# Transposing the first pass's activations on TensorE instead of through HBM

## The chip, the cores and the metric

The kernel runs on the 8 cores of one Trainium2 chip. Each core computes one half of one of the four sequences, 4096 tokens, and no data passes between cores. The metric is the time of one execution in microseconds, set by the slowest core. Lower is better.

## What is computed

The reference is a decoder block on x of shape (4, 8192, 1024):

```
h      = rms_norm(x);  proj = h @ w_in                   # 1024 -> 5888 columns
y_a    = (B * causal_conv3(C * v)) @ w_proj_a            # short gated convolution
y_b    = attention in 3 groups of 4 heads (dilation 1, 4, 16; 128 keys back) @ w_proj_b
x      = x + (sigmoid(g_a) * y_a + sigmoid(g_b) * y_b) @ w_out
h2     = rms_norm(x)
x      = x + (silu(gate) * val) @ w_down                 # gate, val = causal_conv3(h2 @ w_up)
out    = rms_norm(x)
```

A matmul on TensorE sums over partitions. So the normalised rows h, which are made with tokens on partitions, have to be transposed (channels on partitions) before they can be multiplied with w_in.

## The kernel before

Every core works in three passes. **Pass A** (to about 450 us of the trace) normalises the rows, transposes them, projects q, k and v and runs the attention, whose sums go to a tensor `u_d` in HBM. **Pass B**, the mixer (about 450 to 1070 us), projects the convolution's inputs and the gates from the same h, combines the branches and multiplies with w_out. **Pass C** is the gated MLP. TensorE, VectorE (DVE), ScalarE (ACT), GpSimd (POOL) and SyncE (SP) each run their own list of instructions in order, with waits on semaphores. SP issues nearly all DMAs, in order too: while SP waits for one transfer's condition, everything behind it in its list waits. The weights are loaded from POOL's list.

Pass A goes over tiles of 512 tokens in the order 0, -1, -2, 1, E, -3, 2, -4, 3, 4, 5, 6, 7. Tiles 0 to 7 are the core's own tokens. Tiles -4 to -1 and the 16 rows of E lie before them and give only keys and values. A tile is four blocks of 128 rows, and one list `NBL` holds all blocks in order. Each block goes through three steps that are written between the tiles' matmuls:

- `stat(i)`: ACT squares and sums a row (L405), and POOL makes the reciprocal root from it with six small instructions (L319 to L327).
- `mul(i)`: DVE multiplies the block with it (L413) into one of four buffers `hbA`. Then SP issues the x load of block i+4 (L366), which needs the buffer that `mul(i)` has just read, and a store of the block's rows to the HBM tensor `h_d` (L468).
- `back(i)`: brings the block, transposed, into `hTA`, one of four tiles. Two ways exist. For tile 0 and E, `norm_back` runs eight TensorE transposes of 128x128 into one PSUM bank (L425) and one DVE copy out of it (L429). For all other tiles, SP issues one transposing DMA from `h_d` into `hTA` (L484), which waits until the store has landed.

What paces these steps is a counter of ticks: `tick()` is called after each small group of matmuls (usually 8), 20 times in one of the tiles 0 to 7, 16 times in tile -1, 6 or 7 times in -2, -3 and -4. `norm_tick` does at most one `back`, one `mul` and one `stat` in a tick: a new block every 2.4 ticks (every 3.3 from block 24 on), a `mul` at least two ticks after its `stat`, a `back` at least 3 ticks after its `mul` where TensorE transposes and 4 where a DMA does. A tile starts only when its four blocks' `back` steps are written (`need`).

The matmuls of pass A go through L643 (`fm`) and L649 (`tm`). They and `norm_back` take the next of four PSUM banks from `next_ps`; the results leave the banks through `copy` (L256 on ACT, L258 on DVE), and `pick` sends each to the engine with the smaller sum of noted costs. The attention adds scores (L530), exponentials (L533), masks (L537) and products with the values (L556). Group 2's values take a detour through the HBM tensor `v2_d` (`v_d` in the profile: stored at L735, loaded at L740) on SP's list.

Pass B reads h again, from `h_d`, by 33 transposing DMAs of its own (`hb_load`, L984); it needs the rows of tiles 0 to 7 and the last four rows before them. Pass C does the same through `h2_d` (33 more; the profile calls both tensors `h_d`). Pass B transposes its attention output on TensorE in groups of six (L1088).

Of the kernel before, what the change touches and what calls it, by code (L numbers as in the profile page):

```python
# [131 lines left out]
def build_program():  # L132
# [197 lines left out]
    def scale_g(gap, key):  # L330

        S.add("act", lambda e: e.activation(out=gap, in_=gap, func=AF.Copy, scale=float(D) ** 0.5 * RC ** 3 / 2), reads=[key], writes=[key])
# [25 lines left out]
    def emit_xload():  # L358
        i = xload_i[0]
        if i >= len(NBL):  # L360
            return
        xload_i[0] += 1
        t, b = NBL[i]
        n = 16 if t == "E" else 128
        r0, sl = x_row(t, b), i % 4
        S.add("sp", lambda e: e.dma_start(out=xA[sl][0:n, :], in_=x_loc[r0:r0 + n, :]),  # L366
              writes=[("xA%d" % sl,)], dma_sem=sem_x[sl])
# [44 lines left out]
    def norm_mul(xap, xkey, hbap, hbkey, n, gb, gkey, col):  # L412
        S.add("dve", lambda e: e.scalar_tensor_tensor(  # L413
            out=hbap[0:n, :], in0=xap[0:n, :], scalar=rstd[0:n, col:col + 1], in1=gb[0:n, :],
            op0=ALU.mult, op1=ALU.mult), reads=[xkey, ("rstd", col), gkey], writes=[hbkey])
        note("dve", 1450)
# [32 lines left out]
        stamp["s", i] = tickno[0]  # L449

    def by_pe(t):
        return t in ("E", 0)

    def h_row(t, b):
        return 2048 + 512 * t + 128 * b

    def mul(i):
        t, b = NBL[i]
        n = 16 if t == "E" else 128
        if not g1_scaled[0]:  # L460
            g1_scaled[0] = True
            scale_g(g1b, ("g1b",))
        hb, hk = hbA[i % 4], ("hbA%d" % (i % 4),)
        norm_mul(xA[i % 4], ("xA%d" % (i % 4),), hb, hk, n, g1b, ("g1b",), cols_a[i])
        emit_xload()
        if t != "E":
            r0 = h_row(t, b)
            S.add("sp", lambda e: e.dma_start(out=h_d[r0:r0 + 128, :], in_=hb), reads=[hk], writes=[("h_d", t, b)],  # L468
                  dma_sem=sem_ha[i % 4])
        stamp["m", i] = tickno[0]  # L470

    def back(i):
        t, b = NBL[i]
        hk = ("hbA%d" % (i % 4),)
        if t == "E":
            norm_back(hbA[i % 4], hk, 16, hTE, ["hTE"])
            return
        sl = slot_of[t]
        dst, dk = hTA[sl][:, :, b * 128:(b + 1) * 128], [("hTA%d" % sl, b)]
        if by_pe(t):  # L480
            norm_back(hbA[i % 4], hk, 128, dst, dk)
            return
        r0 = h_row(t, b)
        S.add("sp", lambda e: e.dma_start(out=dst, in_=h_d[r0:r0 + 128, :], transpose=True), reads=[("h_d", t, b)],  # L484
              writes=dk, dma_sem=sem_ht[sl][b])

    def norm_tick(force=False):
        if nt[0] < nm[0] and (force or tickno[0] - stamp["m", nt[0]] >= (3 if by_pe(NBL[nt[0]][0]) else 4)) and can_back(nt[0]):
            back(nt[0])
            nt[0] += 1  # L490
        if nm[0] < ns[0] and (force or tickno[0] - stamp["s", nm[0]] >= 2) and nm[0] - nt[0] < 4:
            mul(nm[0])
            nm[0] += 1
        if nt[0] == len(NBL) and 4 in done_tiles and not normed[0]:
            normed[0] = True
            later(1, load_conv)
        ncred[0] = min(ncred[0] + (1 / 2.4 if ns[0] < 24 else PACE), 1.5)
        if ns[0] < len(NBL) and ns[0] - nm[0] < 2 and (force or ncred[0] >= 1):
            ncred[0] -= 1
            stat(ns[0])  # L500
            ns[0] += 1
# [1232 lines left out]
```

## Time and profile before

| | us |
|---|---|
| median of 3 runs (2065.27 to 2070.92) | 2068.2 |
| the profiled execution's own time | 2060.88 |
| its span on the slowest core, 5 | 2059.3 |
| its spans on the other cores | 2039.2 to 2055.6 |

The span runs from a core's first instruction to its last; 1.6 us of the profiled execution lie outside the slowest span. The profiled execution lies 7.3 us under the median. The rows further down are core 5's unless they say core 7. "PE" is TensorE, "PEld" its weight loads, "SPq" the DMA issues of SP. `arena` is the SBUF area that holds nearly all buffers, `psp` is PSUM, `x_loc` the input.

### The profile page before, as it was taken

What the parts mean: (1) busy time and instruction counts of PE and PEld (TensorE: products, weight loads), DVE (VectorE), ACT (ScalarE), POOL (GpSimd) and SP (SyncE); (2) the same over time, 40 slices, a digit from 0 to 9 for tenths busy, and PEclk for the clock granted to TensorE, in tenths of its full rate; (3) what the DMA queues carried; (4) which work ended last, traced back from release to release, by engine and by line L of the source; (5) the groups of instructions that cost most, each with busy time, mean ns of one, the idle gap of its engine ahead of it and who ended that gap; (6) DMA issues with size and microseconds to landing.
All of it is one profiled execution on the core that took longest, in us unless ns stands there. A gap on an engine that the chain in (4) does not pass through costs nothing.

```text
span 2059.3 us, 37750 instructions; the slowest of 8 cores (2039.2 to 2059.3 us)
## 1 busy us (share of the span) xinstructions
PE 1958.0 (95%) x11582; PEld 1011.7 (49%) x11582; DVE 1141.9 (55%) x1774; ACT 811.9 (39%) x1659; POOL 660.5 (32%) x1429
## 2 busy tenths in 40 slices
PE   4789889999999999999999999999999999999998
PEld 2456455655555544444444545555444444444443
DVE  3345454456344445345333938667684867758483
ACT  2344455453222221121222726446462635446361
POOL 2453322001111210110224425445452634445242
PEclk9899999999999999999999999999999999999999
DMA  9999988475333614123449941322313222221201
GB/s 214 167 233 203 218 219 161 102 163 139 112 101 106 118 56 134 39 96 111 62 127 181 197 111 22 103 69 87 112 48 91 74 67 83 57 93 46 83 1 52
DMA packets 224717, 229.54 MB, mean 111 GB/s; under 512 B 123060, under 2 KB 177466, under 8 KB 224136
## 3 DMA queue, kind: packets, MB, share of 16 engines
q1 hardware_dynamic: 182408, 192.73, 34.7%
q0 software_dynamic: 42112, 34.39, 12.2%
q8 instruction: 98, 1.61, 0.3%
q14 instruction: 99, 0.81, 0.1%
HBM read 162.29 MB, written 70.80 MB: 113 GB/s over the span
## 4 chain that ended last, share of the span: by engine, by line
PE 80%; DMA 8%; issue 4%; DVE 3%; POOL 2%; ACT 2%; SPq 1%; DVEq 0%; POOLq 0%; ACTq 0%
PE psp L643 54%; PE psp L1488 14%; PE psp L1243 6%; PE psp L649 3%; DMA h_d<-arena 3%; DMA arena<-w_in 2%; DVE arena L1445 2%; PE psp L556 1%; PE psp L530 1%; SPq L484 1%; ACT arena L1438 1%; ACT arena L405 1%; PE psp L1088 1%; DMA arena<-h_d 0%; DMA arena<-u_d 0%
## 5 line engine op out<-in xcount | busy, mean ns | idle before, releaser
L643 PE MATMUL psp<-arena 128*128 128x512 bf16 (+4 forms) x6848 | 1349.7, 358 | 39.3 <-DMA arena<-h_d 15.3
L643 PEld LDWEIGHTS psp<-arena 128*128 128x128 bf16 x6848 | 660.0, 98 | 689.3 <-issue 55.8
L1445 DVE SCALAR_TENSOR_TENSOR arena<-psp,fcw_s,arena 128x511 f32<-128x511 f32 (+4 forms) x792 | 520.0, 686 | 98.6 <-ACT uc L1436 34.8
L1488 PE MATMUL psp<-arena 128*128 128x512 bf16 x1408 | 308.7, 380 | 5.9 <-POOL arena L1449 2.8
L1438 ACT ACTIVATE arena<-psp,fcb_s,fcw_s 128x512 f32<-128x512 f32 (+1 forms) x396 | 282.8, 733 | 0.0
L1458 POOL TENSOR_TENSOR arena<-arena 128x512 bf16<-128x512 bf16 (+1 forms) x198 | 210.3, 1063 | 76.5 <-ACT uc L1436 48.2
L405 ACT ACTIVATE arena<-arena 128x1024 bf16<-128x1024 f32 (+1 forms) x114 | 120.0, 1053 | 278.4 <-DVE arena L1514 247.2
L1488 PEld LDWEIGHTS psp<-arena 128*128 128x128 bf16 x1408 | 137.8, 98 | 175.0 <-issue 12.4
L1211 DVE TENSOR_TENSOR arena<-psp,arena 128x512 f32<-128x512 f32 (+2 forms) x144 | 90.7, 632 | 219.6 <-PE psp L643 210.9
L1197 ACT ACTIVATE arena<-psp,bg_s 128x512 f32<-128x512 f32 (+2 forms) x144 | 92.0, 640 | 275.0 <-PE psp L643 269.8
L1456 ACT ACTIVATE arena<-arena 128x512 bf16<-128x512 f32 (+1 forms) x198 | 115.4, 583 | 183.2 <-POOL arena L1449 167.8
L1215 POOL TENSOR_TENSOR arena<-arena 128x512 bf16<-128x512 f32 (+2 forms) x72 | 83.5, 1160 | 280.6 <-DVE arena L1211 220.7
L1449 POOL TENSOR_TENSOR arena<-arena,corr 128x2 f32<-128x2 f32 x352 | 89.2, 257 | 179.3 <-DVE arena L1445 166.7
L319 POOL TENSOR_SCALAR ssq<-ssq 128x1 f32<-128x1 f32 (+1 forms) x110 | 27.7, 252 | 366.6 <-ACT arena L405 320.3
L1514 DVE TENSOR_TENSOR arena<-psp,arena 128x512 f32<-128x512 f32 x64 | 43.7, 690 | 178.3 <-PE psp L1488 178.2
L413 DVE SCALAR_TENSOR_TENSOR arena<-arena,rstd 128x1024 bf16<-128x1024 f32 (+1 forms) x82 | 107.0, 1305 | 47.8 <-POOL rstd L327 46.1
L649 PE MATMUL psp<-arena 128*128 128x256 bf16 (+1 forms) x952 | 121.0, 286 | 13.1 <-DMA arena<-h_d 11.2
L256 ACT ACTIVATE arena<-psp 128x512 bf16<-128x512 f32 (+3 forms) x116 | 63.0, 544 | 170.2 <-PE psp L643 114.3
L537 DVE TENSOR_TENSOR arena<-arena,mask 128x1024 bf16<-128x1024 bf16 x96 | 66.1, 689 | 108.1 <-ACT arena L533 108.0
L1243 PE MATMUL psp<-arena 128*128 128x512 bf16 (+1 forms) x528 | 118.1, 382 | 2.5 <-POOL arena L1215 2.5
L533 ACT ACTIVATE arena<-psp 128x1024 bf16<-128x1024 f32 x96 | 96.6, 1020 | 45.8 <-PE psp L530 41.2
L649 PEld LDWEIGHTS psp<-arena 128*128 128x128 bf16 (+1 forms) x952 | 97.0, 106 | 28.0 <-issue 13.8
(85 smaller groups left out, 975.2 us busy)
## 6 DMA issues: line engine op xcount, KB each, us to landing
arena<-x_loc SPq DMA_DIRECT2D x80, 512.0 KB, 5.9
arena<-x_d SPq DMA_DIRECT2D x64, 512.0 KB, 3.7
h_d<-arena SPq DMA_DIRECT2D x80, 256.0 KB, 6.2
x_d<-arena SPq DMA_DIRECT2D x32, 512.0 KB, 3.7
out<-arena SPq DMA_DIRECT2D x32, 512.0 KB, 2.6
u_d<-arena SPq DMA_DIRECT2D x96, 132.0 KB, 5.0
arena<-u_d SPq DMA_DIRECT2D x32, 396.0 KB, 4.1
arena<-w_up POOLq DMA_DIRECT2D x22, 512.0 KB, 14.8
```

The lines of the kernel that those rows point to most:

```text
L405: S.add("act", lambda e: e.activation(out=junk[0:n, :], in_=xap[0:n, :], func=AF.Square, accum_out=ssq[0:n, col:col + 1]), reads=[xkey] + ...
L413: S.add("dve", lambda e: e.scalar_tensor_tensor(out=hbap[0:n, :], in0=xap[0:n, :], scalar=rstd[0:n, col:col + 1], in1=gb[0:n, :], op0=ALU. ...
L533: S.add("act", lambda e: e.activation(out=PA[pi], in_=psp[pr], func=AF.Exp, scale=0.125), reads=[("ps", 2 * pr), ("ps", 2 * pr + 1)], writ ...
L643: S.add("pe", lambda e, kc=kc: e.matmul(out, lhsT=wap[:, kc, col0:col0 + 128], rhs=rhs(kc), start=(kc == 0), stop=(kc == kcn - 1), skip_gr ...
L649: S.add("pe", lambda e, kc=kc: e.matmul(out, lhsT=lhs(kc), rhs=wap[:, kc, c0:c0 + n], start=(kc == 0), stop=(kc == KC - 1), skip_group_che ...
L1197: S.add("act", lambda e, b=b, t=t, br=br: e.activation(out=tmp[t][:, 0:w_], in_=ps[b][:, 0:w_], func=AF.Sigmoid, bias=bg[:, br * 8 + oc:br ...
L1243: S.add("pe", lambda e, b=b, kc=kc, hf=hf: e.matmul(ps[b][0:n, :], lhsT=mT[:, kc, c0:c0 + n], rhs=wO[kc // 4][:, kc % 4, hf * 512:(hf + 1) ...
L1438: S.add("act", lambda e, b=b, t=t, ch=ch, w2_=w2_: e.activation(out=tmpC[t][:, 0:n], in_=ps[b][:, o:w_], func=AF.Identity, scale=w2_, bias ...
L1445: S.add("dve", lambda e, b=b, t=t, sh=sh, wv_=wv_, lo=lo: e.scalar_tensor_tensor(out=tmpC[t][:, lo:n], in0=ps[b][:, o + lo - sh:w_ - sh], ...
L1456: S.add("act", lambda e: e.activation(out=actT[:, p, 0:n], in_=tmpC[tg][:, 0:n], func=AF.Silu), reads=[("tmpC%d" % tg,)], writes=[("actT", ...
L1458: S.add("pool", lambda e: e.tensor_tensor(out=actT[:, p, 0:n], in0=actT[:, p, 0:n], in1=tmpC[tv][:, 0:n], op=ALU.mult), reads=[("tmpC%d" % ...
L1488: S.add("pe", lambda e: e.matmul(ps[b], lhsT=actT[:, k_, bi * 128:(bi + 1) * 128], rhs=wt[:, kk, hf * 512:(hf + 1) * 512], start=(k_ == 0) ...
```

## The change

Every block of pass A is now transposed on TensorE: `by_pe` is true for all tiles, so `back` always calls `norm_back`, three ticks after `mul`, and no transposing DMA (L484) is issued in pass A. The store to `h_d` stays for tiles 0 to 7 and for the last block of tile -1, which pass B reads; tiles -4, -3, -2 and the first three blocks of -1 are no longer stored. Pass B's transposing loads stay as they were.

```
--- before.py
+++ after.py
@@ -449,7 +449,7 @@
         stamp["s", i] = tickno[0]
 
     def by_pe(t):
-        return t in ("E", 0)
+        return True
 
     def h_row(t, b):
         return 2048 + 512 * t + 128 * b
@@ -463,7 +463,7 @@
         hb, hk = hbA[i % 4], ("hbA%d" % (i % 4),)
         norm_mul(xA[i % 4], ("xA%d" % (i % 4),), hb, hk, n, g1b, ("g1b",), cols_a[i])
         emit_xload()
-        if t != "E":
+        if t != "E" and (t >= 0 or (t, b) == (-1, 3)):
             r0 = h_row(t, b)
             S.add("sp", lambda e: e.dma_start(out=h_d[r0:r0 + 128, :], in_=hb), reads=[hk], writes=[("h_d", t, b)],
                   dma_sem=sem_ha[i % 4])
```

## Rows read from the trace of the kernel before

**Rows 1.** The page's first line, and its busy times by engine.

```profile
span 2059.3 us, 37750 instructions; the slowest of 8 cores (2039.2 to 2059.3 us)
...
PE 1958.0 (95%) x11582; PEld 1011.7 (49%) x11582; DVE 1141.9 (55%) x1774; ACT 811.9 (39%) x1659; POOL 660.5 (32%) x1429
```

**Rows 2.** Waits of TensorE, 0 to 500 us: total, times, longest.

```profile
PE psp L643 <- DMA arena<-h_d: 15.3, 2, 13.8
...
PE psp L649 <- DMA arena<-h_d: 11.2, 2, 7.4
...
PE psp L643 <- DMA arena<-w_in: 9.1, 2, 5.8
...
PE psp L556 <- DMA arena<-v_d: 6.0, 1, 6.0
...
PE psp L643 <- ACT arena L256: 2.6, 1, 2.6
```

**Rows 3.** Timeline of SP's queue, tile 3: start, length, what is issued.

```profile
272.88 1.22 SPq L484 DMA_TRANSPOSE arena<-h_d  x1
...
274.79 0.39 SPq L735 DMA_DIRECT2D v_d<-arena  x1
...
280.25 0.32 SPq L740 DMA_DIRECT2D arena<-v_d  x1
```

**Rows 4.** Timeline of ScalarE: start, length, work, [idle before <- releaser].

```profile
207.18 1.06 ACT L405 ACTIVATE arena<-arena 128x1024 bf16<-128x1024 f32 x1 [6.72 <-DMA arena<-x_loc]
```

**Rows 5.** Timeline of TensorE, the work right after its long waits.

```profile
84.44 6.70 PE L643 MATMUL psp<-arena 128*128 128x128 bf16 x32 [13.83 <-DMA arena<-h_d]
...
123.48 7.74 PE L649 MATMUL psp<-arena 128*128 128x256 bf16 x56 [3.78 <-DMA arena<-h_d]
...
208.95 3.31 PE L643 MATMUL psp<-arena 128*128 128x512 bf16 x8 [2.61 <-ACT arena L256]
...
231.23 4.97 PE L649 MATMUL psp<-arena 128*128 128x256 bf16 x24 [7.39 <-DMA arena<-h_d]
...
288.75 3.60 PE L649 MATMUL psp<-arena 128*128 128x256 bf16 x16
```

**Rows 6.** The same view, the mixer: transposes among matmuls.

```profile
586.53 0.50 PE L1088 MATMUL psp<-ident,arena 128*128 128x128 bf16 x6
...
586.86 7.07 PE L1243 MATMUL psp<-arena 128*128 128x512 bf16 x32
```

**Rows 7.** Groups by line, 0 to 500 us: count, busy, mean ns, idle before.

```profile
L425 PE MATMUL psp<-ident,arena 128*128 128x128 bf16 (+1 forms) x40 | 4.4, 277 | 19.1 <-DVE ssq L319 16.6 <-DVE arena L413 2.5
...
L429 DVE COPY arena<-psp 128x1024 bf16<-128x1024 bf16 x4 | 2.7, 683 | 1.3 <-PE psp L425 1.3
```

**Rows 8.** Instructions on h_d: count, ns min/median/max, first and last start.

```profile
L468 SPq DMA_DIRECT2D h_d<-arena x48: 336/424/1527, 11.9 to 331.1; - x48
...
L484 SPq DMA_TRANSPOSE arena<-h_d x44: 1216/1484/6877, 38.9 to 337.9; - x44
```

**Rows 9.** Busy us by engine in one stretch, clock, DMA share, GB/s.

```profile
294.00:448.00 154.00, 153.65 (x1545) 91.84 (x1544) 77.51 (x135) 78.79 (x109) 19.51 (x37) 1.00 0.68 139
```

**Rows 10.** Timeline of VectorE: the multiply of a block of 128 rows.

```profile
68.49 1.28 DVE L413 SCALAR_TENSOR_TENSOR arena<-arena,rstd 128x1024 bf16<-128x1024 f32 x1
...
98.00 1.28 DVE L413 SCALAR_TENSOR_TENSOR arena<-arena,rstd 128x1024 bf16<-128x1024 f32 x1 [2.30 <-POOL rstd L327]
...
101.55 1.28 DVE L413 SCALAR_TENSOR_TENSOR arena<-arena,rstd 128x1024 bf16<-128x1024 f32 x1 [1.34 <-POOL rstd L327]
```

**Rows 11.** Waits of TensorE on core 7, 0 to 500 us.

```profile
PE psp L643 <- DMA arena<-h_d: 12.2, 2, 11.7
...
PE psp L649 <- DMA arena<-h_d: 10.4, 2, 5.4
...
PE psp L556 <- DMA arena<-v_d: 4.2, 1, 4.2
```

**Rows 12.** Span and mean clock of core 7.

```profile
core 7: 2055.6 us, clock 0.985
```

More of the change, by code:

```diff
@@ L451, in by_pe @@
     def by_pe(t):
-        return t in ("E", 0)
+        return True
     def h_row(t, b):
@@ L465, in mul @@
         emit_xload()
-        if t != "E":
+        if t != "E" and (t >= 0 or (t, b) == (-1, 3)):
             r0 = h_row(t, b)
```

## The prediction

> **What bounds the kernel now.** I read the page first, then TensorE's waits in pass A, then what stands behind each of them in the lists of SP and ACT. On the page TensorE is busy for 1958.0 of 2059.3 us [rows 1], so a microsecond is won only where TensorE stands still, and every microsecond of work added to TensorE counts. The waits of pass A show where it stands still: 26.5 us in four waits for transposing loads from h_d (15.3 and 11.2), 9.1 us for weights, 6.0 us for group 2's values and 2.6 us for an eviction on ACT [rows 2].
>
> The last two have the same root. SP's list is in order, and a transposing load in it holds everything behind it until its block's store has landed. At 272.88 us such a load goes out; only then, at 274.79, the store of group 2's values, and their load at 280.25 [rows 3], for which TensorE waits 6.0 us. ACT stands still for 6.72 us until 207.18 because an x load sat in the same list [rows 4]; the eviction behind that `stat` is the one for which TensorE waits 2.6 us. So 26.5 + 6.0 + 2.6 = 35.1 us on core 5 hang on the round trip through h_d.
>
> After each long wait TensorE is also slow. In pass B, at a granted clock of 1.00, the level of 2.4 GHz, 32 matmuls of 512 columns take 7.07 us [rows 6]: 0.22 us each, 0.11 for 256 columns, 0.055 for 128. After the waits the rows read [rows 5]: 6.70 us for 16 matmuls of 128 and 16 of 512 columns (the line names one form), where 4.4 is the full rate; 7.74 for 56 of 256 against 6.2; 3.31 for 8 of 512 against 1.8; 4.97 for 24 of 256 against 2.65; 3.60 for 16 of 256 against 1.8. That is 2.3 + 1.5 + 1.5 + 2.3 + 1.8 = 9.4 us lost at the lower level, 1.2 GHz. Standstill and slow restart together: 44.5 us on core 5.
>
> **The added transposes.** Eleven tiles of four blocks change over: 44 groups of eight transposes on TensorE. The same instruction in pass B shows the cost among matmuls: six start at 586.53, the next matmul starts at 586.86 [rows 6], so 0.055 us each and 0.44 us for eight. 44 x 0.44 = 19.4 us. The lower bound is 18.5, if the first two groups, which fall among the waits for weights in tile 0, cost nothing. The upper is 39, twice 19.4, at the lower of the two clock levels. I take 19.4, since most groups fall where TensorE runs dense.
>
> **The added copies.** 44 copies of 0.68 us [rows 7], 30 us of DVE. In the densest stretch, 294 to 448 us, DVE is busy for 77.51 of 154 us and ACT for 78.79 [rows 9]. The copies also raise DVE's noted cost, so `pick` sends about half as many microseconds of other evictions to ACT. I cost them at nothing, covered by the other three of the four PSUM banks. Without that cover each group would hold TensorE for its copy, 0.68 us, 30 us in all (the slow rival below).
>
> **The removed DMAs.** 44 transposing loads, each holding SP for 1.2 to 6.9 us, and 15 of 48 stores go [rows 8]. The x loads, u_d stores and v2 stores behind them move up. All 35.1 us of waits lose their cause. From below, nothing is left of the gain from SP if the 33 remaining stores, which still wait for DVE, hold it as long; they wait for the same `mul` as the x load ahead of them, so I don't expect that. Two stores and two transposing loads of 256 KB each also vanish from the first 51 us, where TensorE waits 9.1 us for weights [rows 2]: 0 to 9 us, and I take 3, since the weights' own bytes remain.
>
> **The moved wait.** A transposing DMA let TensorE go on with other work; a TensorE transpose that is early stops its whole in-order list, and behind it the evictions and the next `stat`s. Two places matter. Tile -1's last block: its multiply runs from 68.49 to 69.77 [rows 10]. Counting ticks, its transposes come at the last but one tick of tile 0, before a last group of 8 x 0.22 us; tile 0 ends at 84.44 - 13.83 = 70.6 [rows 5], so TensorE is there at about 68.8 and waits 1 us instead of 13.8. Then tiles -1 and -2: multiplies come 3.55 us apart (98.00, 101.55), each just behind POOL's reciprocal root [rows 10]. Tile -1's matmuls at full rate sum to 18.5 us in 16 ticks; with transposes that is some 1.3 us a tick, 3.2 us per block of 2.4 ticks. TensorE is thus 0.35 to 0.6 us per block faster than the chain, over nine blocks 3 to 5 us. I take 6 for both places. Bounds: 0, and 16 if thirteen blocks each wait for the whole multiply, 1.28 us. Later tiles have longer ticks (8 matmuls of 512 columns, 1.8 us, and attention between), so the chain stays ahead.
>
> **The sum, core by core.** Core 5: 44.5 - 19.4 - 6 + 3 = 22.1 us less, 2037.2. But the slowest core counts, and core 5 suffers most now. Core 7 spans 2055.6 [rows 12]; its waits are 12.2 + 10.4 + 4.2 = 26.8 [rows 11], and with slow restarts in core 5's proportion (26.8 x 9.4 / 35.1 = 7.2) 34.0 us. It gains 34.0 - 19.4 - 6 + 3 = 11.6 and ends at 2044.0, after core 5. The slowest span falls by 15.3, the profiled execution from 2060.9 to 2045.6. That execution lay 7.3 us under the median, so the forecast for the median is 2068.2 - 15.3 = 2052.9, or 2053.
>
> **A rule that speaks against it.** The Trainium skill (TensorE: Matmul & The Clock Gate, Part 4) puts a transpose at about 275 ns in a kernel's context. By its figure 352 of them would cost an estimated 97 us instead of 19.4. The mean of 277 ns in tile 0 and E [rows 7] agrees with it as a duration; as a price among matmuls the trace disagrees, since durations overlap there [rows 6].
>
> **Rivals.**
> - *The norm chain paces TensorE.* The wait for h_d becomes a wait for the multiply at its bound of 16 us, with some 2 us of slow restart: 12 us worse, 2065. For it: the 3.55 us pace. Against: it holds for nine blocks only, and the plan leaves three ticks.
> - *Slower: PSUM.* A group of transposes takes one of four banks, and its copy can go to DVE alone, behind multiplies that wait for POOL. If TensorE waits for each copy, 44 x 0.68 = 30 us more: 2083. It decides the sign from 15.3 / 44 = 0.35 us per group. Against it: the half idle DVE [rows 9].
> - *Slower: transposes don't overlap.* At the 0.22 us that one lasts at the full clock (0.50 us for six starting 0.055 apart leaves 0.22 for the last), 352 x 0.22 = 77 us, 58 more: 2111. Against it: the starts 0.055 apart [rows 6]. The page's figure above would end here.
> - *The change does half of what it says.* SP stays clogged by the 33 stores; on core 7 the 4.2 us wait and its restart remain: 2058. Inside the forecast's range.
>
> **How the numbers follow.** Forecast, with its unknown costs (2040 to 2062): 0.77. Norm chain: 0.13. PSUM: 0.08. No overlap: 0.02. A measurement of this kernel can tell about 0.3%, 6.2 us, from no change: 2062.0 to 2074.4. All of the forecast is faster; of the norm chain I give 0.01 to faster, 0.11 to the same and 0.01 to slower; the PSUM case is slower but for 0.02, which a mild form leaves within the bound. So faster 0.78, same 0.13, slower 0.09. For the range I go from 2039 (no new stall, 6 us more from the weights, a little run to run) to 2067, past the norm chain's time; what lies above is the two slower cases and a few hundredths.
>
> **What would show it.** Right: no L484 left in pass A; 392 matmuls at L425 that start some 0.055 us apart; TensorE's wait for h_d below 500 us gone, and with it the waits for v_d and for ACT near 207 us; tile 1 starting some 15 us before 123.5; tile 0's end a few microseconds before 70.6. Wrong: L425 waiting for L413 for more than about 10 us (norm chain); L643 or L649 waiting for L429, or for evictions in the dense stretch that has none now (PSUM); a granted clock below 1.00 between 294 and 448 us; or the slowest core gaining much less than its own waits add up to, which would say that time is lost again in passes B or C.

## The result and the profile after

The changed kernel takes 2043.56 us (median of 4 runs, 2040.35 to 2045.62) against 2066.73 us for the kernel before (4 runs): a ratio of 0.9884, with an interval of 0.9861 to 0.9906. In some executions of every kernel the cores of one die run at a lower granted clock and the time is several per cent longer; the times and ratios in this document are of the other executions. The forecast was 2053, the range 2039 to 2067, and "faster" had 0.78. The profiled execution took 2045.14 us; the forecast for it was 2045.6.

The page of the changed kernel, its first line and TensorE's busy time, answers to [rows 1]:

```profile
span 2043.3 us, 38374 instructions; the slowest of 8 cores (2031.0 to 2043.3 us)
...
PE 1968.3 (96%) x11934; PEld 1028.4 (50%) x11934; DVE 1157.2 (57%) x1790; ACT 824.5 (40%) x1687; POOL 657.7 (32%) x1429
```

TensorE has 352 instructions and 10 us of busy time more, and the span is 16.0 us shorter: what went was standstill, 101.3 us before and 75.0 now. Span and mean granted clock of four cores, to be set beside [rows 12]:

```profile
core 3: 2043.3 us, clock 0.992
...
core 5: 2038.3 us, clock 0.993
core 6: 2041.4 us, clock 0.992
core 7: 2031.0 us, clock 0.996
```

Core 5 gained 21.0 us (22.1 forecast), core 7 24.6 (11.6 forecast), and core 3 is now the last. TensorE's waits on core 5, 0 to 500 us, answer to [rows 2]:

```profile
PE psp L425 <- DVE arena L413: 21.5, 8, 11.5
PE psp L643 <- DMA arena<-w_in: 4.9, 1, 4.9
PE psp L649 <- DMA arena<-w_in: 3.9, 1, 3.9
...
PE psp L643 <- ACT arena L256: 1.0, 1, 1.0
```

No core waits for h_d any more, and none for v_d where before did, near 280 us. Five cores wait 0.3 to 2.3 us for a later load of these values, near 398 us, where before did not wait. The 21.5 us at L425 are mostly the first 25 us of the kernel, where before stood still as well; from 60 to 440 us this wait is 2.5 to 3.2 us on every core, and the wait for the copy at L429 is 0.4. The timeline of TensorE on core 5 shows where, and answers to [rows 5]:

```profile
64.71 0.61 PE L425 MATMUL psp<-ident,arena 128*128 128x128 bf16 x8 [0.92 <-DVE arena L413]
65.15 5.61 PE L643 MATMUL psp<-arena 128*128 128x512 bf16 x24
70.66 0.61 PE L425 MATMUL psp<-ident,arena 128*128 128x128 bf16 x8
...
73.40 0.61 PE L643 MATMUL psp<-arena 128*128 128x128 bf16 x8 [0.40 <-DVE arena L429]
...
84.75 0.61 PE L425 MATMUL psp<-ident,arena 128*128 128x128 bf16 x8 [0.57 <-DVE arena L413]
85.20 0.55 PE L643 MATMUL psp<-arena 128*128 128x16 bf16 x16
...
95.30 0.61 PE L425 MATMUL psp<-ident,arena 128*128 128x128 bf16 x8 [0.64 <-DVE arena L413]
...
99.47 1.89 PE L643 MATMUL psp<-arena 128*128 128x512 bf16 x8 [1.01 <-ACT arena L256]
...
108.97 3.22 PE L649 MATMUL psp<-arena 128*128 128x256 bf16 x28
```

The groups at 64.71 and 70.66 are tile -1's last two blocks. The first of them waits 0.92 us for its multiply, and tile -1 waits 0.40 us at 73.40 for the last copy, where the old kernel waited 13.83 us for the load. The work behind a group starts 0.44 us after it. After a wait of 1.01 us, 8 matmuls of 512 columns take 1.89 us, at a granted clock of 1.00 (99.4 to 101.4 us); after 2.61 us they took 3.31 [rows 5], at 0.57 in the mean (208.9 to 212.3 us). On core 5 the short waits do not bring a slow restart with them. But the same wait of 1.0 to 1.3 us for ACT does on cores 0, 1, 3, 4 and 6, where the same matmuls take 3.2 to 3.5 us. Core 1, whose granted clock is 0.50 from 98.0 to 101.4 us:

```profile
98.48 3.30 PE L643 MATMUL psp<-arena 128*128 128x512 bf16 x8 [1.01 <-ACT arena L256]
```

Tile 1's first matmul is the one at 108.97. The one that started at 123.48 in the kernel before was tile 1's ninth, the first that needs all four blocks; it starts at 109.84 now, 13.6 us earlier.

The same instructions by tile and by line (count, ns min/median/max, first and last start) on core 3; these are the tile h_d, to be set beside [rows 8], and line L425, to be set beside [rows 7]:

```profile
L468 SPq DMA_DIRECT2D h_d<-arena x33: 337/423/823, 11.7 to 306.9; - x33
L984 SPq DMA_TRANSPOSE arena<-h_d x33: 1215/1232/2042, 343.6 to 923.6; - x33
```

```profile
L425 PE MATMUL psp<-ident,arena x392: 164/219/314, 11.5 to 311.0; 128*128 128x128 bf16 x192, 16*128 16x16 bf16 x4
```

L484 is gone from the program. Two stretches of core 3 (us, then busy time with count for TensorE, its weight loads, VectorE, ScalarE and GpSimd, granted clock, DMA share, GB/s):

```profile
70.00:96.00 26.00, 24.28 (x216) 16.75 (x214) 15.58 (x19) 11.57 (x23) 18.10 (x47) 1.00 0.51 152
...
300.00:440.00 140.00, 136.18 (x1330) 82.64 (x1328) 62.89 (x105) 61.68 (x89) 9.75 (x17) 0.99 0.68 125
```

In the first stretch the granted clock stays at 1.00 among the transposes, and TensorE still stands still for 1.7 us of 26. The second stretch holds only the last two groups; its 0.99 comes from core 3's wait of 2.26 us for v_d, after which 16 matmuls of 256 columns take 3.18 us (400.68).

To see where the time was won, I take six moments from TensorE's timeline of each core and average them over the eight cores (us). The end of tile -1 is taken at the first of its last 48 matmuls, which have two columns each and take 1.3 us in all. The start of pass B is taken, here and below, at the first line of the timeline that shows matmuls of 388 columns; the first of them lies 3.0 us before it in every profile.

```
                          before   after   difference of the stage ending here
first matmul of tile 0      26.4    28.4    +2.0
first matmul of tile -1     83.0    73.0   -12.0
end of tile -1             102.2    95.4    +3.2
first matmul of E          158.9   147.5    -4.6
first matmul of pass B     442.3   426.8    -4.2
end of the span           2050.8  2038.6    +3.3
```

Pass A ends 15.6 us earlier. The largest part comes from one place, the wait ahead of tile -1. Passes B and C, which the change does not touch, took 3.3 us more in this pair.

### The profile page after: what moved, and what is told of

It is laid out like the page before. It is cut to its first block, busy times and chain, and to the rows that moved or that the text cites. A ratio compares the mean times of both kernels' runs of the same rounds, so it can differ in the third digit from the quotient of the medians.

```text
span 2043.3 us, 38374 instructions; the slowest of 8 cores (2031.0 to 2043.3 us)
## 1 busy us (share of the span) xinstructions
PE 1968.3 (96%) x11934; PEld 1028.4 (50%) x11934; DVE 1157.2 (57%) x1790; ACT 824.5 (40%) x1687; POOL 657.7 (32%) x1429
## 4 chain that ended last, share of the span: by engine, by line
PE 85%; DMA 4%; DVE 4%; issue 3%; ACT 2%; POOL 2%; SPq 0%; DVEq 0%; POOLq 0%; ACTq 0%
PE psp L643 58%; PE psp L1488 14%; PE psp L1243 5%; PE psp L649 4%; DMA arena<-w_in 2%; DVE arena L1445 2%; PE psp L556 1%; PE psp L530 1%; PE psp L425 1%; PE psp L1088 1%; DMA arena<-u_d 1%; ACT arena L405 0%; POOL rtmp L325 0%; DMA arena<-x_loc 0%; ACT arena L1438 0%
## 5 line engine op out<-in xcount | busy, mean ns | idle before, releaser
L256 ACT ACTIVATE arena<-psp 128x512 bf16<-128x512 f32 (+2 forms) x144 | 75.7, 529 | 148.9 <-PE psp L643 96.9
L649 PE MATMUL psp<-arena 128*128 128x256 bf16 (+1 forms) x952 | 116.2, 276 | 5.1 <-DMA arena<-w_in 4.2
```

Of the source, the lines that this page charges most:

```text
L649: S.add("pe", lambda e, kc=kc: e.matmul(out, lhsT=lhs(kc), rhs=wap[:, kc, c0:c0 + n], start=(kc == 0), stop=(kc == KC - 1), skip_group_che ...
```

## The experiments

Each ratio is against the kernel before on the same chip. The first four kernels shared a chip.

**All stores kept.** After, but with all 48 stores to h_d.

```
-        if t != "E" and (t >= 0 or (t, b) == (-1, 3)):
+        if t != "E":
```

> The changed kernel, but all 48 stores to h_d are issued again (15 of them are read by nothing). Theory 'round trip' (the gain is TensorE no longer waiting for store, landing and transposing load): the stores wait for the same multiply as the x load ahead of them, so 2 us at most are lost, all before tile 1: about 0.989 of before, 2044 to 2046 us. Rival 'DMA relief' (the gain comes from fewer bytes on the DMA engines in pass A): 15 of the 59 transfers that went away come back, so about a quarter of the gain goes: 2049 us or more, with TensorE's wait for w_in longer by several us.

2042.93 us, 0.9883 (0.9865 to 0.9901), beside 0.9884 for after; pass B starts at 426.5 us in the mean over the cores, after 426.8. The 15 stores left out are worth nothing that can be measured, and the rival of fewer DMA bytes, which put this kernel at 2049 us or more, falls as far as these stores go.

**Only the early tiles by TensorE.** Tiles -3, 2, -4 and 3 to 7 go back to transposing loads, and the rows of tiles -3 and -4 are stored again for them.

```
     def by_pe(t):
-        return True
+        return t in ("E", 0, -1, -2, 1)
...
-        if t != "E" and (t >= 0 or (t, b) == (-1, 3)):
+        if t != "E" and (t >= 0 or (t, b) == (-1, 3) or not by_pe(t)):
```

> TensorE transposes only tiles 0, E, -1, -2 and 1; tiles -3, 2, -4 and 3 to 7 go through h_d and the transposing load again, as in the kernel before, and are stored. By the sum of the prediction: the early waits (13.8, 1.5 and 3.8 us on core 5) with their slow restarts go, 12 groups of 0.44 us and some 3 us of waits for the multiply come, net 16 us less than before; the later tiles' waits (7.4 for h_d, 2.6 and 6.0 behind SP's list, with 5.6 of slow restart) stay, their 32 groups of transposes (14 us) are saved, so all in all 2048 to 2054 us, 0.992, and TensorE's waits for h_d and v_d show up again between 200 and 290 us. Rival 'only the first tile counts': the later waits shrink by themselves since the tiles come earlier and SP is less full; then the saved transposes make it faster than the changed kernel, 2035 us or less.

2053.85 us, 0.9934 (0.9910 to 0.9959). Waits of TensorE on core 1, 60 to 440 us:

```profile
PE psp L649 <- DMA arena<-h_d: 16.2, 2, 8.2
PE psp L556 <- DMA arena<-v_d: 8.7, 2, 7.3
PE psp L425 <- DVE arena L413: 3.2, 5, 0.9
```

E starts 5 us earlier than in after (142.5 against 147.5), and pass B 8.8 us later (435.6). The wait for the load comes back where the load comes back (14.7 us in the mean over the cores), and v_d's wait with it (4.8). The early tiles alone give a bit more than half of the gain.

**The transposes twice.** The eight transposes of the 44 new groups are issued twice, into the same bank with the same result.

```
-        for kc in range(KC):
+        for kc in list(range(KC)) * (1 if dst is hTE or first else 2):
...
-            norm_back(hbA[i % 4], hk, 128, dst, dk)
+            norm_back(hbA[i % 4], hk, 128, dst, dk, t == 0)
```

`first` is a new argument of `norm_back`, so that tile 0 and E stay as they were; the next experiment has it too.

> The changed kernel with each of the 44 groups of eight transposes issued twice into the same bank (the second writes the same values). The price of a transpose among matmuls: 352 more at 0.055 us give 19.4 us, 2063 us, about the time of the kernel before. Rival, the price is the duration (0.22 us at the full clock, or the page's 275 ns): 77 to 97 us more, 2120 us and up. Rival, groups partly hide in TensorE's other waits: clearly under 15 us more.

2056.57 us, 0.9944 (0.9924 to 0.9963): 0.0060 above after's ratio, about 12.5 us. Pass B starts 10.1 us later than in after. Core 6, timeline and one stretch of it (columns as above):

```profile
84.62 1.06 PE L425 MATMUL psp<-ident,arena 128*128 128x128 bf16 x16
85.51 0.55 PE L643 MATMUL psp<-arena 128*128 128x16 bf16 x16
```

```profile
70.00:96.00 26.00, 25.79 (x272) 20.03 (x273) 15.26 (x19) 12.13 (x24) 17.17 (x46) 1.00 0.56 160
```

Sixteen transposes hold TensorE for 0.89 us, 0.056 each, as the row of the mixer said. But tile -1, in which seven groups are doubled, 3.1 us at that price, lasts 23.4 us where it lasted 22.4 with half as many: TensorE is busy for 25.79 us of the 26 that had 1.7 us of standstill in after, so most of the second set fills a wait there. The second set of 352 transposes costs 10 to 12.5 us, 0.23 to 0.28 us for a group, and not the 44 x 0.44 = 19.4 that were expected. (The 10 are the shift of pass B's start, although tile 0's first matmul came 2.0 us earlier than in after; the 12.5 are the difference in time.) The cost is not spread evenly: from E to pass B 24 groups cost 8.0 us, 0.33 each, and the 20 before them 4.2. That the first set costs what the second does is taken over from this, not shown. By the 275 ns that the Trainium skill gives for a transpose (TensorE: Matmul & The Clock Gate, Part 4) it would be an estimated 97 us; the run disagrees, by a factor of eight to ten.

**The copies twice.** The copy out of PSUM is made twice for the same groups.

```
-        S.add("dve", lambda e: e.tensor_copy(out=dst, in_=src), reads=[("ps", t)], writes=dkeys)
+        for _ in range(1 if dst is hTE or first else 2):
+            S.add("dve", lambda e: e.tensor_copy(out=dst, in_=src), reads=[("ps", t)], writes=dkeys)
```

> The changed kernel with each of the 44 copies out of PSUM made twice, 30 us more of VectorE work, each between a bank's filling and its release. If the copies are covered by the other three banks, as the prediction costs them: 0 to 4 us more, 2044 to 2048 us. If TensorE waits for banks (the prediction's slower rival): 0.68 us for most of the 44, 20 to 30 us more, 2064 us or more, with waits of L643, L649 or L530 for L429.

2045.18 us, 0.9892 (0.9877 to 0.9907): 30 us more work on VectorE cost about 2 us. TensorE's waits on core 5, 60 to 440 us, where the copy is now line 430:

```profile
PE psp L644 <- DVE arena L430: 1.5, 2, 0.9
...
PE psp L650 <- DVE arena L430: 0.7, 1, 0.7
```

The single copy is hidden, as forecast; the PSUM rival falls.

**Group 2's values: the stores, then the whole way, off SP's list.** Two changes to the kernel before. First the stores of v2 (L735) go out on GpSimd's queue; then, on another chip, their load (L740) too.

```
-        later(1, lambda: S.add("sp", lambda e: e.dma_start(out=dst, in_=V2n[i].rearrange("p (q h) e -> p q (h e)", q=2)),
+        later(1, lambda: S.add("gq", lambda e: e.dma_start(out=dst, in_=V2n[i].rearrange("p (q h) e -> p q (h e)", q=2)),
...
-        S.add("sp", lambda e: e.dma_start(out=V2[s % 2].rearrange("p r h e -> p r (h e)"),
+        S.add("gq", lambda e: e.dma_start(out=V2[s % 2].rearrange("p r h e -> p r (h e)"),
```

> The kernel before, with one thing changed: the stores of group 2's values go out from POOL's list instead of SP's, so that no transposing load stands ahead of them. If SP's list is what makes TensorE wait for v_d (3.9 to 6.0 us in the profiles of before), that wait falls below 2 us and about 4 to 8 us with the slow restart are gained: 2059 to 2064 us; the waits for h_d stay at 20 to 27 us. Rival: the wait is the length of the way itself (copy, store, landing, load of 8 us); then it stays and the time is that of before, or a little over it for the issues on POOL.

> The kernel before, with the stores and the loads of group 2's values both issued from POOL's list. With the stores alone there, they went out at 259 and 264 us, but the load stayed on SP until 272, behind a transposing load at 267, and TensorE still waited. If SP's list is the cause, the load now goes out at about 270 or earlier and TensorE's wait for v_d falls below 1 us on most cores (3.6 us mean before); 2 to 5 us are gained on the cores' mean span, less what POOL loses by waiting for the stores to land. If it is the length of the way, the wait stays at 3 us or more.

Stores alone: 2060.35 us, 0.9993 (0.9975 to 1.0010). Both: 2069.7 us, 1.0010 (0.9982 to 1.0037). Neither moves the time, and both expectations by which SP's list is the cause missed. The wait for v_d, in the mean over the cores, was 3.7 us in before; it is 2.4 with the stores on GpSimd and 3.6 with both. GpSimd's queue on core 5 in the second run:

```profile
262.23 0.79 POOL L735 DMA_DIRECT2D v_d<-arena  x1 [0.19 <-issue]
...
267.17 0.79 POOL L735 DMA_DIRECT2D v_d<-arena  x1 [0.19 <-issue]
...
276.48 0.57 POOL L740 DMA_DIRECT2D arena<-v_d  x1 [8.51 <-DMA v_d<-arena]
```

TensorE gets its values only then, 11.7 us after the load went out:

```profile
288.14 0.60 PE L556 MATMUL psp<-arena 128*128 128x66 bf16 x8 [4.84 <-DMA arena<-v_d]
```

SP holds nothing of this way, and the way is still too long: 9.3 us from the last store to the load, 11.7 us from the load to TensorE. But the run does not clear SP's list either, since GpSimd's queue has a price of its own. In the mean over the cores the two last stores of these values are 7.5 us apart in before, 4.9 with the whole way on GpSimd and 4.1 in after; from the last store to the load it takes 5.7, 8.2 and 6.8 us. So the stores came closer together and the rest of the way got longer: 13.2 us from the first of the two stores to the load in before, 13.1 with the way on GpSimd, 11.0 in after. What made the wait go in after is not settled.

**The last tiles back to loads.** After, with two or three late tiles by transposing loads, where TensorE runs dense and a load has long ticks to come in.

```
     def by_pe(t):
-        return True
+        return t not in (6, 7)
```

and, run on two chips,

```
     def by_pe(t):
-        return True
+        return t not in (5, 6, 7)
```

> The changed kernel, but the blocks of tiles 6 and 7, which are ready long before TensorE needs them, come through h_d and the transposing load again (their rows are stored anyway). Eight groups of transposes go away, at the 0.3 us per group that the doubled transposes cost, or at 0.44: 2.4 to 3.5 us less than the changed kernel, 2040 to 2041, with no wait for h_d in pass A. Rival: SP's list is clogged again, x loads or u_d stores behind these loads make something wait: no gain, or 2046 and more, with waits for h_d, v_d or x loads after 270 us.

> As the one before, for tiles 5, 6 and 7: twelve groups less, 3.6 to 5.3 us, so 2038 to 2040 if nothing waits. But tile 5's loads stand in SP's list when group 2's values of tile 3 are stored: if SP's list is what counts, the wait for v_d comes back with 4 to 6 us and its slow restart, and the time is 2042 to 2046.

> The variant that transposes tiles 5, 6 and 7 by DMA again, for a comparison with the changed kernel on one chip. Twelve groups of transposes less, 3.6 to 5.3 us by the prices measured so far: ratio to before lower by 0.002 to 0.003 than the changed kernel's. If SP's list is clogged by these loads after all: equal or slower.

The first gave a ratio of 0.9916 (0.9883 to 0.9949), which settles nothing: three of its executions took 2034.0 to 2036.1 us and three 2049.3 to 2054.8, and in the profile, one of the longer three, cores 6 and 7 have a lower granted clock than the other six and start pass B some 17 us after them. Span and clock of three cores:

```profile
core 4: 2024.8 us, clock 0.997
...
core 6: 2047.7 us, clock 0.979
core 7: 2046.1 us, clock 0.982
```

On cores 0 to 3 of this profile, all at 0.992 to 0.995, pass B starts at 419.2 us in the mean, and no core waits for h_d.

The second gave 2034.7 us, 0.9886 (0.9854 to 0.9919), on a chip where the kernel before takes 2060.2, and 2038.6 us, 0.9857 (0.9839 to 0.9874), on another, where after ran beside it with 0.9876 (below): 0.0019 better, about 4 us, with intervals that overlap. Pass B starts at 418.2 and 422.4 us, after's at 426.2 to 426.8. TensorE waits for h_d on no core in either run. The wait for v_d did not come back (0.6 us on one core of sixteen), although tile 5's loads stand in SP's list then and the two stores of group 2's values are 5.8 and 6.0 us apart, not 4.1: this speaks against SP's list alone as its cause. From the first matmul of E to pass B, where the twelve groups are gone, it takes 271.2 us where after, on the same chip, takes 276.3: 5.1 us, 0.43 for a group, and 6.0 on the other chip against the first after. For these late tiles that is the full price of 0.44, not 0.23 to 0.28.

**The kernel before and after, again.** No edit. The first ran on the chip of v2's stores, of the two late tiles and of the first run with three, the second on a third chip, beside v2's whole way and the second run with three.

> The kernel before, unchanged, for a second profile and its spans by core. If the first profiled execution (2060.9, where the median is 2067) was a quick draw: slowest core 2062 to 2068 us, and the cores differ by 10 us or more at the start of pass B, where the changed kernel's differ by 8 and that with doubled transposes by 3. Ratio 1.000.

> The changed kernel, unchanged, beside kernels that vary it and beside before on one chip. The forecast was a fall of 15.3 us in the slowest span, the first comparison gave 23.2. If the forecast's terms are right and only its starting point (the profiled execution of before) was a quick one: the mean over the cores' spans falls by 12 to 17 us where before's mean span is near 2051, and by 20 to 24 where it is near 2059, and the cores lie closer together than before's (slowest less mean 3 to 6 us against 7 to 10). If a term was mis-sized by 8 us: 20 to 24 us of the mean fall everywhere.

Before: 2059.56 us, 1.0001 (0.9988 to 1.0015). After: 2043.2 us, 0.9876 (0.9861 to 0.9891). These two say how far a kernel varies. Mean over the cores of the moment at which pass B starts, in each profile: kernels with before's loads 442.3, 441.9 (v2's stores moved), 439.6 (again) and 446.6 (v2's whole way moved), so 7.0 us apart; kernels with all tiles on TensorE 426.8, 426.5 (all stores) and 426.2, so 0.6 us apart. The waits for h_d below 500 us in the first four: 23.6, 20.9, 22.7 and 26.4 us. None of the last three ran beside a before of about 2060 us, and the kernel with three late tiles by loads, which waits for no load, started pass B 4.2 us earlier on the chip where before is that quick than on the third chip.

**Late tiles by loads, and half the reciprocal roots on VectorE.** Every second reciprocal root of blocks 8 to 23, whose multiplies TensorE waits for in tiles -1 and -2, goes from GpSimd to VectorE.

```
-        cols_a[i] = norm_stat(xA[i % 4], ("xA%d" % (i % 4),), junk, ("junk",), n, "dve" if i < 4 else "pool")
+        cols_a[i] = norm_stat(xA[i % 4], ("xA%d" % (i % 4),), junk, ("junk",), n, "dve" if i < 4 or (8 <= i < 24 and i % 2) else "pool")
...
-        return True
+        return t not in (5, 6, 7)
```

> The same, with every second reciprocal root of blocks 8 to 23 made on DVE instead of POOL. If TensorE is paced by the chain of norms in tiles -1 and -2 (3.5 us a block, roots on POOL), the waits of L425 for L413 after tile 0 (2 to 3 us in all) go and tile -1 lasts 19 to 20 us instead of 22.4; 2 to 3 us are gained. If tile -1 lasts as long because of its own matmuls and transposes, nothing changes, and DVE's longer list may cost 1 us.

2034.9 us, 0.9837 (0.9823 to 0.9852): the lowest ratio of all, 0.0039 under after's on the same chip (8 us). But tile -1 lasts 21.6 us, where 19 to 20 were expected and after has 22.4, and the wait for the multiply, 0.9 to 1.4 us now, has a successor. Waits of TensorE on core 2, 0 to 440 us:

```profile
PE psp L643 <- DVE arena L429: 2.1, 1, 2.1
...
PE psp L649 <- DVE arena L429: 1.4, 1, 1.4
```

TensorE now waits for VectorE's copies, 3.5 us here, where it was 0.4 in after. Pass B starts at 419.3 us, between the two runs of the version without the roots (418.2 and 422.4), so nothing shows that the roots help; what is shown is that the whole is faster than after.

## Why the prediction was right, and where it was off

**The mechanism held.** What was forecast as the sign of it is there: L484 gone, 392 transposes at L425, 0.056 us apart among matmuls, tile 1's ninth matmul 13.6 us earlier (15 forecast), no wait for h_d below 500 us, and TensorE's wait for ACT near 207 gone (the 1.0 us at 99.47 is another one). ACT's waits for x loads from 100 to 300 us, 14.1 us on core 5 and 3.3 to 10.7 on the others, are gone on every core too. Where the waits went the granted clock rose: from 60 to 420 us it is 0.94 to 0.97 in before, core by core, and 0.99 to 1.00 in after. The moved wait ahead of tile -1 was put at 1 us and is 0.92, one block earlier, and 0.40 for the copy.

**The norm chain** was forecast at 6 us for both places; it is 2.5 to 3.2. The rival (16 us) fell: TensorE waits for four or five blocks, each time under 1 us. What the term left out is a wait for ACT in tile -2, 1.0 to 1.3 us on every core, with a slow restart behind it on five of the eight.

**The transposes** were mis-sized: 19.4 us against the 10 to 12.5 measured for a second set of the same number. The price of one among matmuls was right (0.056 us), and in the late tiles a group costs about what was forecast (0.33 to 0.43 us); wrong was to charge all 44 groups at it and, in a term of its own, the waits for the multiply. In tile -1 those two are in part the same microseconds: what a group takes there shortens the wait that follows. The 277 ns of [rows 7], which the prediction set beside the rule against it, are a mean of two shapes, mostly 311 ns for 128x128 in tile 0 and 164 for E's; among the 392 of after the median is 219. The copies at nothing were right.

**The weights** were to give 3 us. The waits for w_in fell, in the mean over the cores, from 10.3 to 8.5 us, but tile 0's first matmul came 2.0 us later, so that nothing is left. The sign named for it failed as well: tile 0 was to end a few microseconds before 70.6 and ends, on core 5, at 73.0. Whether the late start is the change's doing is open: in the profiles of its variants this moment lies between 25.9 and 29.3 us.

**The wait for v_d** near 280 us went on all eight cores, 3.7 us in the mean. But the reason given, that SP's list holds the stores, is not shown: with the whole way off that list the wait stays, though the way is then no shorter, and with tile 5's loads back in the list it does not return. That step is open, and so is the new wait near 398 us, 0.8 us in the mean, which the forecast did not have. On core 3 it brings one of the signs named for a wrong forecast, a granted clock below 1.00 between 294 and 448 us, in small.

**Core by core** the forecast held for core 5 and failed for core 7, which was to be the last. Pass A became 9.4 us (core 3) to 25.1 us (core 5) shorter. What follows it, from the start of pass B to the end, ran from 1602.8 to 1614.6 us over the cores of the two profiles, with the same instructions: 12 us that no wait of pass A explains, so the last core can't be told from pass A's waits.

**The size of the gain.** The slowest span fell by 16.0 us between the two profiles, where 15.3 were forecast; between the medians it is 23.2. The step that failed is the last one, where the fall worked out for one execution was taken off the median as it stood. The profiles suggest that what varies from execution to execution is in good part what the change removes: pass B starts between 439.6 and 446.6 us in profiles with before's loads, and within 0.6 us in three without. So in a slower execution there would be more to remove, and the profiled one was among the quick. In the profiled pair the mean core span fell by 12.2 us, from 2050.8 to 2038.6, and on the third chip by 22.2, from 2059.8 to 2037.6, with after at nearly the same place; a term that was 8 us too small would have shown in both. With the prices of the runs the sum can be made to come out: on the third chip the waits for h_d and v_d are 26.4 + 3.6 = 30.0 us (in the profile with v2's way on GpSimd, which left the time as it was); with the slow restarts in core 5's proportion, 44.5 / 35.1, 38.0; less 12.5 for the transposes and 2.8 for the multiply, 22.7. It is no proof, since these waits are of one execution of another kernel, the quickest of its kind, and with 10 for the transposes it gives 25.2. The cores also differ less there: the slowest lies 7.9 us above the mean in before and 3.5 in after, which is about the rest of the fall, 25.5 us between the medians. By the same prices the profiled pair, with 23.6 + 3.7 us of waits, would give 34.6 - 12.5 - 2.8 = 19.3 us at the start of pass B, by the forecast's own 34.6 - 19.4 - 6 + 3 = 12.2, and 15.6 were measured. The 3.7 us to 19.3 stay open; the wait for ACT in tile -2 with its slow restarts, some 2 us in the mean, may be part of them. Passes B and C then took 3.3 us longer, so that the forecast came so near to this pair is partly luck. After never ran beside a before of about 2060 us, which would have tested the account.

## What to carry to other kernels

A round trip through memory that TensorE waits for may be worth more than one trace shows: here its waits differed from core to core and from execution to execution, and the slowest core sets the time. When TensorE gets new work where it already waits, charge the work or the wait, not both. And change only the tiles whose wait shows in the timeline: three late tiles whose loads nothing waited for were as well or better left to the queues (about 4 us, with intervals that overlap).

## What the runs showed of the hardware

Passes B and C took 1602.8 to 1614.6 us from core to core with the same instructions, at mean granted clocks of 0.984 to 0.996 for the whole span. The kernel before took 2060.2 us on one chip, and 2066.7, 2066.7 and 2068.7 in three other series of runs, while the one without transposing loads in pass A stayed at 2042.9 to 2043.6 in three series, each beside a before of 2066.7 us or more. The wait for h_d differed between the cores of one execution by 9 us (19.6 on core 0, 28.8 on core 2). On core 5 a store of 132 KB from GpSimd's queue and the load of 1,056 KB behind it took 9.3 and 11.7 us; from the last store to the load it took 8.2 us on that queue in the mean over the cores, and 5.7 and 6.8 us on SP's in before and after. A group of eight transposes takes 1.01 us in the first 25 us, after waits of 2.5 to 11.5 us, and 0.61 us later, and the next matmul of a dense stretch starts 0.44 us after the group did.
